# Plain 32-bit products for the first layer's queries, keys and values, in place of three products of rounded halves

## The chip, the cores and the metric

The kernel runs on one core of one Trainium2 chip. The metric is device time in microseconds of that core; the median of three runs before the change is 1491.33 us (1490.42 to 1494.95).

## The reference, cut to what matters

The reference is one inference step of a two-layer encoder for 512 prompt tokens and 64 new tokens (T = 576 rows of 1024 features). The first layer mixes tokens with eight forgetting-attention ("fox") heads and eight stick-breaking ("sb") heads of 64 features that share one input projection; the second layer uses latent attention; both are followed by a mixture of 32 experts. The change touches the input projection of the first layer alone:

```python
def ab_project(h, w_in, b_f):
    z = h @ w_in                       # (T x 1024) @ (1024 x 3080), float32
    qa, ka, va, f_logit, qb, kb, vb = jnp.split(z, cuts, axis=-1)
    logf = jax.nn.log_sigmoid(f_logit + b_f)
    ...
def sb_attend(q, k, v, pos_q, pos_k):  # 4 of 8 head pairs
    z = jnp.einsum('bqhd,bkhd->bhqk', q, k) * (HEAD_DIM ** -0.5)
    log_beta = jnp.where(before, jax.nn.log_sigmoid(z), NEG_INF)
    log_rest = jnp.where(before, jax.nn.log_sigmoid(-z), 0.0)
    later = lax.cumsum(log_rest, axis=log_rest.ndim - 1, reverse=True) - log_rest
    return jnp.einsum('bhqk,bkhd->bqhd', jnp.exp(log_beta + later), v)
```

## The kernel before

All of the work is one program of stages: the first attention (`attend` with `mla` false, from the start to about 366 us), its output product and mixture of experts, a combining stage, the latent attention, and the second mixture. Inside a stage each engine runs its own in-order list of instructions, and semaphores join them; `hold` is a wait followed by a count that every engine keeps.

`attend` takes heads two at a time: pairs 0 to 3 are stick-breaking, 4 to 7 fox. A pair is ten units (two heads by five blocks of queries, `unit_of`). For each unit TensorE computes scores, ScalarE, VectorE and GpSimd turn them into probabilities (`soften`, `softplus`, `cut`, `stick`, `exponent` for sb; `decay`, `logits`, `exponent`, `even` for fox), TensorE transposes those (`turn`), ScalarE copies the transposes out (`turn_out`), and for every two units TensorE multiplies by the values (`values`), whose result VectorE copies into `mix` (`finish`, L936). Scores run three units ahead in sb pairs and four in fox pairs.

The projections of pair p+1 are woven into pair p on TensorE (`project_ab`): `AB_AFTER` says after which unit each half of a projection stands, q0 ahead of unit 0, q1 after unit 0, k0 after 2, k1 after 3, the transposes of the keys (kt) after 4, v0 after 5, v1 after 7, the transposes of the values (vt) after 8. Each of the six product blocks is four slices of features by two halves of the 576 tokens, so 8 products of a 128x128 weight slice by 128x288 of tokens. They are made by `split_matmul`, three fp32r products: rounded weights by rounded tokens (L199), rounded weights by the low part of the tokens (L200), low part of the weights by rounded tokens (L201). The results lie in two PSUM banks, so a block of the next projection waits (`banks_free`) until ScalarE and VectorE have copied the last one out (`copy_out`: q1, k1, kt, v1, vt).

The halves come from `split`: ScalarE rounds a whole 128x1024 weight tile (`w_hi`, L189) and VectorE subtracts (`w_lo`, L193). `splits` places these after unit 1 (values of p+1), unit 4 (queries of p+2) and unit 8 (keys of p+2); so pair 6 has only the one after unit 1, and pair 7 none. The tokens are split once at the start (`split_x_hi`, `split_x_lo`). Ahead of pair 0 its own projections run with no attention beside them; the forget gates (`Gates`) use that time too.

SyncE issues the loads: `load_w(p, n)` puts a weight tile into its one buffer `wp[n]` once the tile before it has been split, and `load_past` the cached keys and values.

Of the kernel before, what the change touches and what calls it, by code (L numbers as in the profile page):

```python
# [209 lines left out]
class Gates:  # L210
# [4 lines left out]
    def __init__(self, k):  # L215
        self.k, self.nc = k, k.nc
        sem = lambda n: new_signal(k, f"g_{n}")

        flat = lambda a: a.rearrange("p j n -> p (j n)")
        room_a, room_b = flat(k.w_gu[0][0]), flat(k.w_gu[1][0])  # L220
        self.logf, self.cum, self.ones = (room_a[0:HEADS, n * KEYS:(n + 1) * KEYS] for n in range(3))
        self.low = room_a[0:HEADS, 3 * KEYS:3 * KEYS + T]
        self.t_abs, self.t_exp = (room_b[0:HEADS, n * T:(n + 1) * T] for n in range(2))
        self.t_ln = self.t_abs
        at = 2 * T
        self.tok = room_b[:, at:at + NT * HEADS].rearrange("p (t h) -> p t h", t=NT)
# [11 lines left out]
        self.out, self.tok_t, self.tok_e, self.cum_ready, self.x_hi_done, self.x_lo_done = (  # L238
            sem(n) for n in ("out", "tok_t", "tok_e", "cum_ready", "x_hi_done", "x_lo_done"))
        self.z = banks(k, 0, 2)[0:HEADS, 0:T]  # L240
        self.trans = banks(k, 2, 1)


    def load(self, sp):
        k = self.k
        sp.dma_start(self.wf, k.w_f).then_inc(self.f_in, 16)
        for b in range(2):
            sp.dma_start(k.xT[:, 4 * b:4 * b + 4, 0:T], k.x_t[:, 4 * b:4 * b + 4, :]).then_inc(self.xt_in[b], 16)
        sp.dma_start(self.bf, k.b_f).then_inc(self.f_in, 16)
# [46 lines left out]
    def products(self, pe):  # L296
        nc, k, z = self.nc, self.k, self.z
        pe.wait_ge(self.f_in, 48)
        for j in range(J):
            if j % 4 == 0:  # L300
                pe.wait_ge(self.xt_in[j // 4], 16)
            nc.tensor.matmul(z[:, 0:SEQ], self.wf[:, j, :], k.xT[:, j, 0:SEQ], start=(j == 0), stop=(j == J - 1))
            last = nc.tensor.matmul(z[:, SEQ:T], self.wf[:, j, :], k.xT[:, j, SEQ:T], start=(j == 0), stop=(j == J - 1))
        last.then_inc(self.z_ready, 1)
        pe.wait_ge(self.filled, 2)
        pe.wait_ge(self.x_lo_done, J)

# [10 lines left out]

    def split_x_hi(self, act):
        for j in range(J):  # L320
            if j % 4 == 0:
                act.wait_ge(self.xt_in[j // 4], 16)
            split_hi(self.nc, self.k.x_hi[:, j, :], self.k.xT[:, j, 0:T]).then_inc(self.x_hi_done, 1)

    def logs(self, act):
# [7 lines left out]


    def split_x_lo(self, dve):
        for j in range(J):
            dve.wait_ge(self.x_hi_done, j + 1)
            split_lo(self.nc, self.k.x_lo[:, j, :], self.k.xT[:, j, 0:T], self.k.x_hi[:, j, :]).then_inc(self.x_lo_done, 1)

# [39 lines left out]
def attend(k, mla, m, gates=None):  # L379
# [6 lines left out]
    with ExitStack() as c:  # L386
# [16 lines left out]
        else:  # L403
            wp = k.wp

            w_hi = [sb(f"w_hi{a}", [P, J, P]) for a in range(2)]
            w_lo = [sb(f"w_lo{a}", [P, J, P]) for a in range(2)]

            room = k.xT[:, :, :].rearrange("p j n -> p (j n)")
# [13 lines left out]
        else:  # L423
            names = ("zeroed hi0 hi1 hi2 lo0 lo1 lo2 kp_in0 kp_in1 vp_in0 vp_in1 cumk_in0 cumk_in1 cumq_ready projected proj_act proj_dve k_out v_out "
                     "scores_ready scored bias_ready bias_step probs_ready probsT_ready probsT_used o_ready o_done "
# [46 lines left out]
        with nc.Block() as block:  # L472
# [3 lines left out]
            def _(sp):  # L476
                row = lambda a, at: a[bass.ds(at, 1), :, :].rearrange("a p n -> p (a n)")

                def load_w(p, n):

                    if mla:
# [31 lines left out]
                def pair(p, par, kind, more):  # L513
# [23 lines left out]
                else:  # L537
                    gates.load(sp)
                    load_past(0, 0, False)
                    for n in range(3):  # L540
                        load_w(1, n)
                    store(0, 0, "sb", 0)
                    gates.store(sp)
                    store(0, 0, "sb", 1)
# [11 lines left out]
            def _(pe):  # L556
# [5 lines left out]
                def project_ab(p, par, step):  # L562
# [11 lines left out]
                    if half == 0:  # L574
                        banks_free(p, (0, 1, 3)[n], (s[f"lo{n}"], p + 1))
                    for j in range(4 * half, 4 * half + 4):
                        for b in range(2):
                            at = slice(b * HT, (b + 1) * HT)
                            last = split_matmul(nc, halves[:, b, :], (w_hi[(par + n) % 2][:, j, :], w_lo[(par + n) % 2][:, j, :]),
                                                (k.x_hi[:, j, at], k.x_lo[:, j, at]),  # L580
                                                j == 0, j == J - 1)
                    if half:
# [109 lines left out]

            def splits(split, p, par, u):

                if mla:
                    return
                last = lambda ahead: isinstance(p, int) and p + ahead >= PAIRS
                if u == 1 and not last(1):
                    split(p + 1, 1 - par, 2)
                if u == 4 and not last(2):  # L700
                    split(p + 2, par, 0)
                if u == 8 and not last(2):
                    split(p + 2, par, 1)

            def first_copies(split, copy_out, gates_part):

                if not mla:
                    split(0, 0, 0)
                    split(0, 0, 1)
                    gates_part()  # L710
                for step in copied:
                    copy_out(0, 0, step)
                    if not mla:
                        {"q1": lambda: split(0, 0, 2), "k1": lambda: split(1, 1, 0), "v1": lambda: split(1, 1, 1)}.get(step, lambda: None)()


            @block.scalar
            def _(act):
                nc.scalar.preload_act_table_set("natural_log_exp_and_others")
                if not mla:  # L720
                    gates.split_x_hi(act)
                act.wait_ge(s["zeroed"], n_zeroed)
                copy = lambda dst, src, scale=1.0: nc.scalar.activation(dst, src, ACT.Copy, scale=scale)  # L723

                def copy_out(p, par, step):
# [24 lines left out]
                    last.then_inc(s["proj_act"], 1)  # L750

                def split(p, par, n):

                    used = STEPS * (p - 1) + (2, 4)[n] if n < 2 else STEPS * p + 1
                    waits = [] if isinstance(p, int) and p == 0 and n < 2 else [(s["projected"], used)]
                    hold(act, passed, (s[f"w{n}_in"], 16 * (p + 1)), *waits)
                    split_hi(nc, w_hi[(par + n) % 2][:], wp[n][:]).then_inc(s[f"hi{n}"], 1)

# [34 lines left out]
                def pair(p, par, kind, more):  # L793
# [11 lines left out]
                    for u in range(UNITS):  # L805
# [5 lines left out]
                        copies(u)  # L811
                        splits(split, p, par, u)

                first_copies(split, copy_out, lambda: gates.logs(act))
                each_pair(act, pair)


            @block.vector
            def _(dve):
# [12 lines left out]
                dve.wait_ge(s["zeroed"], n_zeroed)  # L832
                if not mla:
                    gates.split_x_lo(dve)

# [14 lines left out]
                def copy_out(p, par, step):  # L850
# [35 lines left out]
                    if step == "q4":  # L886
                        rotate(p)

                def split(p, par, n):
                    hold(dve, passed, (s[f"hi{n}"], p + 1))  # L890
                    split_lo(nc, w_lo[(par + n) % 2][:], wp[n][:], w_hi[(par + n) % 2][:]).then_inc(s[f"lo{n}"], 1)

# [45 lines left out]
                def pair(p, par, kind, more):  # L938
# [23 lines left out]
                    for u in range(UNITS):  # L962
# [12 lines left out]
                        copies(u)  # L975
                        splits(split, p, par, u)
                    finish(p, NT - 1, kind)

                first_copies(split, copy_out, lambda: gates.sums(dve))
                if not mla:  # L980
# [1215 lines left out]
def stream_step(nc, dram):  # L2196
    with ExitStack() as ctx:
        k = Core(nc, ctx, dram)
        with ExitStack() as c:
            sb = lambda n, s, d=F32: c.enter_context(nc.sbuf_tensor(n, s, d))  # L2200
            k.wp = [sb(f"w_{n}", [P, J, P]) for n in "qkv"]
            k.wp_in = [new_signal(k, f"w_{n}_in") for n in "qkv"]
            k.x_hi, k.x_lo = sb("x_hi", [P, J, T]), sb("x_lo", [P, J, T])
            attend(k, False, None, Gates(k))
# [92 lines left out]
```

## Time and profile before

| | |
|---|---|
| median of 3 runs | 1491.33 us |
| profiled execution's own time | 1488.06 us |
| its span, first to last instruction | 1486.2 us |
| TensorE matmul busy | 1200.4 us, 81% |
| VectorE busy | 675.6 us, 45% |
| ScalarE busy | 434.9 us, 29% |
| mean granted TensorE clock | 0.92 of full speed |

The profile comes from one execution. Engines are named PE (TensorE matmul), PEld (its weight loads), DVE (VectorE), ACT (ScalarE), POOL (GpSimd) and SP (SyncE). A matmul record has a start and a modelled duration; matmuls are pipelined, so neighbouring records overlap, and the pace of a stream is read from one start to the next. A full 32-bit matmul leaves two records. "Idle before" is the time from the end of the last record on that engine to the start of this one, and what follows "<-" is what ended it; "issue" means that nothing in the profile did.

### The profile page before, as it was taken

The numbers are of one execution on the slowest core, as the hardware profiler recorded it, in microseconds if no ns is written. First come the engines' busy times: TensorE is split into PE (matmuls) and PEld (weight loads), VectorE is DVE, ScalarE is ACT, GpSimd is POOL, SyncE is SP. The second block draws the span as 40 slices with busy tenths as digits, with TensorE's granted clock in tenths as the row PEclk, the third lists the DMA queues.
The fourth block names the chain that finished last, engine by engine and source line by source line (L and its number), as shares of the span: only waits on it lengthen the run. The fifth ranks groups of instructions, "written<-read, shape, count | busy, mean of one in ns | idle before, by whom it ended". The sixth has DMA issues, their size and how long they took to land. (4 is left out here: it accounts for less than half of the span.)

```text
span 1486.2 us, 24147 instructions
## 1 busy us (share of the span) xinstructions
PE 1200.4 (81%) x8148; PEld 829.6 (56%) x8148; DVE 675.6 (45%) x1855; ACT 434.9 (29%) x985; POOL 238.0 (16%) x370
## 2 busy tenths in 40 slices
PE   6887888996994998778479699999799499777750
PEld 4766677774873554434245567676587355444420
DVE  4455664444563442222164355556656345222217
ACT  3455664335200211101022144444621021101102
POOL 1111112222012222111100000000001223112116
PEclk9999999998995999999779899999999599999985
DMA  4222123422539999999560210000033999999945
GB/s 164 75 62 72 30 95 103 160 61 77 213 142 368 376 360 380 379 373 398 189 221 1 92 70 15 29 16 15 29 133 135 366 374 355 358 378 388 394 191 189
DMA packets 61382, 290.80 MB, mean 196 GB/s; under 512 B 12689, under 2 KB 23121, under 8 KB 44257
## 3 DMA queue, kind: packets, MB, share of 16 engines
q1 hardware_dynamic: 49408, 265.90, 48.5%
q0 software_dynamic: 10560, 18.90, 4.0%
q10 hardware_dynamic: 1312, 4.72, 0.8%
q8 instruction: 56, 0.92, 0.3%
q14 instruction: 46, 0.37, 0.1%
HBM read 275.91 MB, written 29.29 MB: 205 GB/s over the span
## 5 line engine op out<-in xcount | busy, mean ns | idle before, releaser
L1745 PE MATMUL psum<-w_gu,moe_xgT 128*64 128x256 f32 x1968 | 259.8, 408 | 71.9 <-DMA w_gu<-in_w_gate_up 54.4
L1745 PEld LDWEIGHTS psum<-w_gu,moe_xgT 128*64 128x64 f32 x1968 | 153.8, 145 | 162.3 <-issue 115.2
L199 PE MATMUL psum<-x_hi,ab_w_hi 128*128 128x288 f32 x384 | 125.5, 327 | 7.4 <-ACT ab_k_tok L723 4.7
L1792 ACT ACTIVATE moe_silu<-psum 64x256 f32<-64x256 f32 x64 | 24.2, 378 | 338.8 <-PE psum L1745 294.1
L1816 DVE COPY moe_xgT<-psum 128x512 f32<-128x512 f32 x64 | 44.3, 692 | 164.1 <-PE psum L1735 163.2
L201 PE MATMUL psum<-x_hi,ab_w_lo 128*128 128x288 f32 x384 | 115.4, 301 | 0.0
L200 PE MATMUL psum<-x_lo,ab_w_hi 128*128 128x288 f32 x384 | 115.4, 300 | 0.0
L1694 POOL DMA_INDIRECT y_d<-mix,moe_slots x60 | 55.5, 925 | 363.5 <-DVE mix L1829 357.5
L1762 PE MATMUL psum<-w_dn,moe_hidT 128*64 128x512 f32 x352 | 85.1, 604 | 2.2 <-issue 2.2
L1824 DVE COPY moe_hidT<-psum 128x128 f32<-128x128 f32 x64 | 18.7, 292 | 144.3 <-PE psum L1753 142.8
L199 PEld LDWEIGHTS psum<-x_hi,ab_w_hi 128*128 128x128 f32 x384 | 74.3, 193 | 13.5 <-issue 11.8
L1797 ACT ACTIVATE mix<-psum 64x512 f32<-64x512 f32 x64 | 37.7, 589 | 134.8 <-PE psum L1762 134.8
L200 PEld LDWEIGHTS psum<-x_lo,ab_w_hi 128*128 128x128 f32 x384 | 74.1, 193 | 3.8 <-issue 2.4
L201 PEld LDWEIGHTS psum<-x_hi,ab_w_lo 128*128 128x128 f32 x384 | 73.7, 192 | 0.0
L199 PE MATMUL psum<-mix_w_hi,mix_mix_hi 128*128 128x512 f32 (+1 forms) x160 | 65.0, 406 | 9.7 <-DVE mix_w_lo L193 9.7
L1829 DVE COPY mix<-psum 64x512 f32<-64x512 f32 x64 | 44.4, 694 | 52.4 <-PE psum L1762 52.4
L632 PE MATMUL psum<-ab_kT,ab_q 128*128 128x128 f32 (+4 forms) x160 | 64.5, 510 | 4.2 <-DVE cum_tok L361 2.5
L780 ACT ACTIVATE mla_probs<-mla_score,mla_small 128x128 f32<-128x128 f32 (+4 forms) x80 | 48.3, 603 | 58.0 <-DVE mla_small L901 57.0
L201 PE MATMUL psum<-mix_w_hi,mix_mix_lo 128*128 128x512 f32 (+1 forms) x160 | 63.5, 397 | 0.0
L200 PE MATMUL psum<-mix_w_lo,mix_mix_hi 128*128 128x512 f32 (+1 forms) x160 | 63.5, 397 | 0.0
L1683 POOL DMA_INDIRECT mix<-x_d,moe_tokens x54 | 51.0, 945 | 61.0 <-issue 58.7
L632 PE MATMUL psum<-mla_kh,mla_q 96*128 96x128 f32 (+4 forms) x160 | 59.7, 479 | 0.9 <-DVE mla_q L872 0.9
(307 smaller groups left out, 2182.3 us busy)
## 6 DMA issues: line engine op xcount, KB each, us to landing
w_gu<-in_w_gate_up SPq DMA_DIRECT2D x54, 2048.0 KB, 34.9
w_dn<-in_w_down SPq DMA_DIRECT2D x44, 1024.0 KB, 36.8
xT<-in_w_down SPq DMA_DIRECT2D x20, 1024.0 KB, 40.1
w_gu<-in_w_gate_up SPq DMA_DIRECT2D x10, 1536.0 KB, 40.6
w_gu<-in_w_out SPq DMA_DIRECT2D x4, 2048.0 KB, 8.5
combine_ys<-y_d SPq DMA_DIRECT2D x16, 512.0 KB, 8.2
xT<-in_w_gate_up SPq DMA_DIRECT2D x10, 512.0 KB, 42.8
xT<-cum_d SPq DMA_DIRECT2D x8, 544.0 KB, 6.8
```

The lines of the kernel that those rows point to most:

```text
L199: nc.tensor.matmul(dst, r32(ah), r32(bh), start=first, stop=False)
L200: nc.tensor.matmul(dst, r32(ah), r32(bl), start=False, stop=False)
L201: return nc.tensor.matmul(dst, r32(al), r32(bh), start=False, stop=last)
L632: last = nc.tensor.matmul(slot(u)[0:rows, 0:min(width, BANK)], q, key[:, 0:min(width, BANK)], start=True, stop=True)
L780: nc.scalar.activation(at_unit(probs, u)[0:rows], at_unit(score, u)[0:rows], ACT.Exp, scale=-1.0, bias=small[0:rows, u % NT, 0:1], accum_o ...
L1683: pool.indirect_dma_start(out=xg[n], out_offset=None, in_=k.x_d[:, :], in_offset=bass.IndirectOffsetOnAxis(ap=idx, axis=0), bounds_check=T ...
L1694: pool.indirect_dma_start(out=k.y_d[:, :], out_offset=bass.IndirectOffsetOnAxis(ap=idx, axis=0), in_=yo[n], in_offset=None, bounds_check=2 ...
L1745: last = nc.tensor.matmul(gu(s)[h * CB:(h + 1) * CB, 0:EH], xgT[:, s, j, :], gate_up_tile(k.w_gu[n], j)[:, h * EH:(h + 1) * EH], start=(j ...
L1762: last = nc.tensor.matmul(y(s)[h * CB:(h + 1) * CB, :], hidT[:, s, j, :], w_dn[n][:, j, h * BANK:(h + 1) * BANK], start=(j == 0), stop=(j ...
L1797: nc.scalar.activation(yo[n][:, 0:BANK], y(s)[0:CB, :], ACT.Copy).then_inc(y_act, 1)
L1816: nc.vector.tensor_copy(xgT[:, s, :, :].rearrange("p j q -> p (j q)"), xtr(s)).then_inc(xgT_ready, 1)
L1829: nc.vector.tensor_copy(yo[n][:, BANK:D], y(s)[CB:P, :]).then_inc(y_dve, 1)
```

## The change

The fp32r halves of the tokens and weights go, with their buffers and semaphores. The tokens are loaded into a tile of their own, `x_in_t`, and the weights are read in `wp`, where the DMA puts them; each product is one full 32-bit matmul. A weight buffer comes free when TensorE has used it, so its reload waits for the count `projected`; the reload of the value weights moves behind the store of the keys on SyncE's queue. The gates' part on ScalarE and VectorE moves from ahead of the first copy out to behind the copy q1.

```diff
     def load(self, sp):
-            sp.dma_start(k.xT[:, 4 * b:4 * b + 4, 0:T], k.x_t[...])
+            sp.dma_start(k.x_in_t[:, 4 * b:4 * b + 4, :], k.x_t[...])
     def products(self, pe):              # the gates read k.x_in_t too
-        pe.wait_ge(self.x_lo_done, J)
-    def split_x_hi(self, act):           # both functions gone
-    def split_x_lo(self, dve):
 def attend(k, mla, m, gates=None):
-            w_hi = [sb(f"w_hi{a}", [P, J, P]) for a in range(2)]
-            w_lo = [sb(f"w_lo{a}", [P, J, P]) for a in range(2)]
                 def load_w(p, n):
-                    hold(sp, passed, (s[f"lo{n}"], p))
+                    hold(sp, passed, (s["projected"], STEPS * (p - 1) + (1, 2, 4)[n]))
                 def pair(p, par, kind, more):        # SyncE
                     load_past(p + 1, 1 - par, kind == "fox")
-                    for n in range(3):
+                    for n in range(2):
                         if not last_w:
                             load_w(p + 2, n)
                     store(p + 1, 1 - par, kind, 0)
+                    if not last_w:
+                        load_w(p + 2, 2)
                     store(p + 1, 1 - par, kind, 1)
                 def project_ab(p, par, step):        # TensorE
                     if half == 0:
-                        banks_free(p, (0, 1, 3)[n], (s[f"lo{n}"], p + 1))
+                        banks_free(p, (0, 1, 3)[n], (s[f"w{n}_in"], 16 * (p + 1)))
                     for j in range(4 * half, 4 * half + 4):
                         for b in range(2):
-                            last = split_matmul(nc, halves[:, b, :], (w_hi[...][:, j, :], w_lo[...][:, j, :]),
-                                                (k.x_hi[:, j, at], k.x_lo[:, j, at]), j == 0, j == J - 1)
+                            last = nc.tensor.matmul(halves[:, b, :], wp[n][:, j, :], k.x_in_t[:, j, at], start=(j == 0), stop=(j == J - 1))
-            def splits(split, p, par, u):            # and split() on ScalarE and VectorE
-                if u == 1 and not last(1):
-                    split(p + 1, 1 - par, 2)
-                if u == 4 and not last(2):
-                    split(p + 2, par, 0)
-                if u == 8 and not last(2):
-                    split(p + 2, par, 1)
-            def first_copies(split, copy_out, gates_part):
-                    split(0, 0, 0); split(0, 0, 1); gates_part()   # written on three lines
+            def first_copies(copy_out, gates_part):
                 for step in copied:
                     copy_out(0, 0, step)
-                        # after q1: split(0, 0, 2), after k1: split(1, 1, 0), after v1: split(1, 1, 1)
+                    if step == "q1":
+                        gates_part()
```

## Rows read from the trace of the kernel before

**Rows 1.** The page's costliest groups: line, tiles, count | busy us, mean ns | idle before

```profile
L199 PE MATMUL psum<-x_hi,ab_w_hi 128*128 128x288 f32 x384 | 125.5, 327 | 7.4 <-ACT ab_k_tok L723 4.7
...
L201 PE MATMUL psum<-x_hi,ab_w_lo 128*128 128x288 f32 x384 | 115.4, 301 | 0.0
L200 PE MATMUL psum<-x_lo,ab_w_hi 128*128 128x288 f32 x384 | 115.4, 300 | 0.0
```

**Rows 2.** TensorE's waits, pairs 0 to 3: waiting tile, releaser, total us, times, longest

```profile
PE psum L570 <- ACT ab_vT L723: 8.5, 4, 2.1
PE psum L657 <- DVE mix L936: 5.8, 4, 1.9
PE psum L644 <- ACT w_gu L777: 5.0, 4, 2.2
PE psum L199 <- ACT ab_k_tok L723: 4.7, 4, 1.2
PE psum L570 <- DVE ab_kT L877: 3.1, 4, 0.8
PE psum L644 <- ACT ab_probsT L723: 2.6, 4, 0.8
...
PE psum L632 <- DVE ab_score L920: 1.7, 4, 0.4
PE psum L644 <- issue: 1.1, 4, 0.3
```

**Rows 3.** The same view, pairs 4 to 7 (229.6 to 366.1 us)

```profile
PE psum L644 <- issue: 4.9, 8, 0.8
PE psum L657 <- DVE mix L936: 3.8, 2, 1.9
PE psum L644 <- DVE w_gu L930: 3.1, 1, 3.1
...
PE psum L570 <- DVE ab_vT L882: 0.8, 3, 0.3
```

**Rows 4.** TensorE's timeline in a product block of pair 0: start us, us

```profile
61.73 0.29 PE L200 MATMUL psum<-x_lo,ab_w_hi 128*128 128x288 f32 x1
...
64.14 0.30 PE L200 MATMUL psum<-x_lo,ab_w_hi 128*128 128x288 f32 x1
```

**Rows 5.** Timeline, full 32-bit products of the forget gates (512 and 64 columns)

```profile
16.83 1.02 PE L302 MATMUL psum<-xT,w_gu 128*8 128x512 f32 x2
17.69 0.27 PE L303 MATMUL psum<-xT,w_gu 128*8 128x64 f32 x2
```

**Rows 6.** Timeline, the latent projection: 128 columns, each with a 128x128 load

```profile
801.15 1.61 PE L2136 MATMUL psum<-mix,xT 128*128 128x128 f32 x13
```

**Rows 7.** Start of pair 0's own projections and of its scores, TensorE's timeline

```profile
38.30 0.37 PE L199 MATMUL psum<-x_hi,ab_w_hi 128*128 128x288 f32 x1 [1.63 <-DVE ab_k_tok L881]
48.91 0.35 PE L632 MATMUL psum<-ab_kT,ab_q 128*128 128x128 f32 x1 [2.54 <-DVE cum_tok L361]
```

**Rows 8.** VectorE's timeline in pair 1

```profile
108.71 1.23 DVE L193 TENSOR_TENSOR ab_w_lo<-w_v,ab_w_hi 128x1024 fp32r<-128x1024 f32 x1 [0.91 <-ACT ab_w_hi L189]
109.85 0.95 DVE L918 TENSOR_TENSOR_SCAN ab_bias<-ab_ones,ab_score 128x384 f32<-128x384 f32 x1
...
136.49 1.23 DVE L193 TENSOR_TENSOR ab_w_lo<-w_k,ab_w_hi 128x1024 fp32r<-128x1024 f32 x1 [1.37 <-ACT ab_w_hi L189]
137.63 0.28 DVE L936 COPY mix<-psum 128x128 f32 x1
```

**Rows 9.** Timeline, the last values of pair 6, which has no split after unit 8

```profile
343.93 0.80 PE L657 MATMUL psum<-ab_probsT,ab_v_all 128*64 128x64 f32 x20 [0.55 <-issue]
```

**Rows 10.** Stretches: us, busy (instructions) of PE, PEld, DVE, ACT, POOL, granted clock, DMA

```profile
94.00:98.00 4.00, 4.00 (x19) 3.82 (x19) 0.81 (x3) 2.79 (x9) 0.58 (x2) 0.57 0.72 211
...
870.00:900.00 30.00, 29.14 (x206) 20.68 (x204) 17.11 (x62) 13.79 (x40) 0.00 (x0) 1.00 0.08 20
```

More of the change, by code:

```diff
@@ L237, in __init__ @@
             sem(n) for n in ("f_in", "filled", "consts", "z_ready", "act_step", "dve_step"))
-        self.out, self.tok_t, self.tok_e, self.cum_ready, self.x_hi_done, self.x_lo_done = (
-            sem(n) for n in ("out", "tok_t", "tok_e", "cum_ready", "x_hi_done", "x_lo_done"))
+        self.out, self.tok_t, self.tok_e, self.cum_ready = (sem(n) for n in ("out", "tok_t", "tok_e", "cum_ready"))
         self.z = banks(k, 0, 2)[0:HEADS, 0:T]
@@ L301, in products @@
                 pe.wait_ge(self.xt_in[j // 4], 16)
-            nc.tensor.matmul(z[:, 0:SEQ], self.wf[:, j, :], k.xT[:, j, 0:SEQ], start=(j == 0), stop=(j == J - 1))
-            last = nc.tensor.matmul(z[:, SEQ:T], self.wf[:, j, :], k.xT[:, j, SEQ:T], start=(j == 0), stop=(j == J - 1))
+            nc.tensor.matmul(z[:, 0:SEQ], self.wf[:, j, :], k.x_in_t[:, j, 0:SEQ], start=(j == 0), stop=(j == J - 1))
+            last = nc.tensor.matmul(z[:, SEQ:T], self.wf[:, j, :], k.x_in_t[:, j, SEQ:T], start=(j == 0), stop=(j == J - 1))
         last.then_inc(self.z_ready, 1)
         pe.wait_ge(self.filled, 2)
-        pe.wait_ge(self.x_lo_done, J)
     def turn(self, pe):
@@ L316, in turn @@
         last.then_inc(self.tok_t, 1)
-    def split_x_hi(self, act):
[L320 to L323, printed above, removed]
     def logs(self, act):
@@ L539, in _ @@
                     load_past(0, 0, False)
-                    for n in range(3):
-                        load_w(1, n)
+                    load_w(1, 0)
+                    load_w(1, 1)
                     store(0, 0, "sb", 0)
+                    load_w(1, 2)
                     gates.store(sp)
@@ L691, in attend @@
             after_of = MLA_AFTER if mla else AB_AFTER
-            def splits(split, p, par, u):
-                if mla:
-                    return
-                last = lambda ahead: isinstance(p, int) and p + ahead >= PAIRS
-                if u == 1 and not last(1):
-                    split(p + 1, 1 - par, 2)
-                if u == 4 and not last(2):
-                    split(p + 2, par, 0)
-                if u == 8 and not last(2):
-                    split(p + 2, par, 1)
-            def first_copies(split, copy_out, gates_part):
[L707 to L710, printed above, removed]
+            def first_copies(copy_out, gates_part):
                 for step in copied:
                     copy_out(0, 0, step)
-                    if not mla:
-                        {"q1": lambda: split(0, 0, 2), "k1": lambda: split(1, 1, 0), "v1": lambda: split(1, 1, 1)}.get(step, lambda: None)()
+                    if step == "q1":
+                        gates_part()
             @block.scalar
@@ L719, in _ @@
                 nc.scalar.preload_act_table_set("natural_log_exp_and_others")
-                if not mla:
-                    gates.split_x_hi(act)
                 act.wait_ge(s["zeroed"], n_zeroed)
@@ L750, in copy_out @@
                     last.then_inc(s["proj_act"], 1)
[L752 to L757, printed above, removed]
                 def soften(p, u):
@@ L811, in pair @@
                         copies(u)
-                        splits(split, p, par, u)
-                first_copies(split, copy_out, lambda: gates.logs(act))
+                first_copies(copy_out, lambda: gates.logs(act))
                 each_pair(act, pair)
@@ L832, in _ @@
                 dve.wait_ge(s["zeroed"], n_zeroed)
-                if not mla:
-                    gates.split_x_lo(dve)
                 def rotate(p):
@@ L975, in pair @@
                         copies(u)
-                        splits(split, p, par, u)
                     finish(p, NT - 1, kind)
-                first_copies(split, copy_out, lambda: gates.sums(dve))
+                first_copies(copy_out, lambda: gates.sums(dve))
                 if not mla:
```

15 lines of the change are left out of this document (3 added, 12 removed).

## The prediction

> **What bounds the kernel now.** I read four views. The page's costliest groups say how much TensorE time the products take: 3 x 384 records, 356 us of modelled busy time [rows 1]; that is 8 sets of projections, each of 6 blocks of 8 products, so 24 records a block. The timeline of one block gives the real pace: 18 records from 61.73 to 64.14 us, 0.134 us each, 3.21 us a block [rows 4]. The view of who waited for whom then says who sets the end, and here the stage has two halves. In the four stick-breaking pairs (48.9 to 229.6 us, 45.2 us a pair) TensorE stands idle 32.5 us, 8.1 us a pair, and nearly every wait ends on ScalarE or VectorE [rows 2]: a chain over three engines and TensorE take turns at being last. In the fox pairs the only large waits are VectorE's copy L936 in two pairs, a latency marked "issue", and one start of pair 7 that has no projection beside it [rows 3]: TensorE is the bound, and what a product costs is paid in full. Behind 366 us nothing is touched; that part starts later or earlier as a whole.
>
> **The price of a product.** A full 32-bit product leaves two records: 512 columns take 17.69 - 16.83 = 0.86 us, 0.43 each, or 0.84 ns a column and record [rows 5]. Those weights have 8 columns. With a 128x128 load ahead of each record and only 128 columns, 13 records take 1.61 us, at most 0.124 each [rows 6], so the load is almost hidden even there. For 288 columns no row exists. By columns from [rows 5] it is 0.242 us a record; on a line between 0.124 at 128 and 0.43 at 512 it is 0.252. I take 0.244, near the first, since 512 columns leave more cover than 128 and 288 is over twice the latter. A product then takes 0.488 us against 3 x 0.134 = 0.402, a block 3.90 against 3.21: **+0.69 us a block** (0.66 to 0.82), 4.14 us a set, 33 us of TensorE over 48 blocks (32 to 39). So for TensorE alone the change is a loss; three fp32r passes were cheaper than one full product.
>
> Two rules of the Trainium skill bear on this. "TensorE: Matmul & The Clock Gate", section "Back-to-back issue gap", gives a warm single pass N/2.4 + 2.5 ns, an estimate of 122.5 ns for 288 columns; "FP8 and Floating Point Precision", section "TensorE Precision Notes", counts four passes in a true 32-bit product. By those a product goes from 368 to 490 ns, 47 us over 384 products instead of 33. The fp32r row is slower than the first rule [rows 4], so the trace disagrees with it and the sum goes by the rows.
>
> **The lead-in (pair 0's own projections, to 48.9 us).** Six blocks with nothing beside them: +4.1. Before, v0 waits 1.63 us for VectorE's key copy, which stands behind a 1.2 us split; with the split gone ScalarE's part of that copy is last, about 0.9 us after the transposes: -0.7. The first scores wait 2.54 us for the last copies of the gates [rows 7], also behind a split: -1.2 to -1.3. The gates' part now runs behind copy q1, inside the k blocks, which with 7.8 us are longer than its some 6 us (uncovered it would cost those 6). Sum **+2.1** (0 to +4.1, or -1 if the copies end earlier than I think).
>
> **Stick-breaking pairs.** ScalarE loses three roundings and VectorE three subtractions of 1.23 us in each pair. They are not idle filler: the scan of a unit starts at 109.85, right behind a subtraction that itself waited 0.91 us for its rounding, and the copy L936 at 137.63 right behind another [rows 8]. I walk once round a pair, with +0.69 at each of six blocks (+4.2 with the cold start of q0), and take off what each wait in [rows 2] gives back (it can give back 0.1 to 0.3 more than its idle time, the tail of the record before it):
> - Ahead of the first transposes (w_gu, 1.25 us a pair): its chain starts with the first scores and doesn't depend on q0; the longer q0 hides in it. -0.8.
> - kt (ab_kT, 0.78): VectorE reaches the copy some 1.2 us after k1 ends because the split after unit 1 has pushed its queue; now the copy starts at once. -0.9.
> - v0 (ab_k_tok, 1.18): the scan of unit 6 and the softening of unit 7 come after the key copies and the later scores, and so move with TensorE. -0.2.
> - Scores of unit 9 (ab_score, 0.43): behind the split after unit 4. -0.7.
> - Transposes of unit 7 (ab_probsT, 0.65): ScalarE is through with unit 7's exponent early. -0.9.
> - vt (ab_vT, 2.1): a chain of scores 9, softening, scan, cut and exponent, which has moved with TensorE by the same amount. -0.2.
> - Last values (mix, 1.45): the subtraction is gone; pair 6, which has no split after unit 8, shows what stays, 0.55 [rows 9]. -1.35, from the usual 1.9.
>
> Sum 4.2 - 5.05 = **-0.85 a pair, -3.4 for four**. Bounds: if only the first of these gives back, +3.4 a pair, +13.6; if all idle but the 0.27 "issue" and the 0.55 goes, 4.2 - 7.3 = -3.1, -12.4 for four. The walk lies between because about half of the wait time hangs on scores that TensorE now delivers later.
>
> **Fox pairs.** Pairs 4, 5 and 6 carry projections: +4.14 each. The copy L936 gives back 1.89 - 0.55 = 1.34 in pairs 4 and 5 [rows 3, 9], nothing in 6. The waits for vT (0.26) and "issue" are latencies with no block between cause and wait, and stay. Pair 7 is as before. Sum **+9.7** (9 to 12).
>
> **Queues and loads.** A weight tile is now asked for after q1, k1 or v1 instead of after its split, and is needed at the same step one pair on, most of 40 us later; the value tile is asked for behind the key store, which waits for kt and so for less than v1. I cost it at nothing; late by the whole, it would show as a wait of q0, k0 or v0 on a DMA. The start's token splits lie beside the gate products, whose end at 20.87 lets q0 go at once: nothing.
>
> **The clock.** Behind the idle time at a pair's end the granted clock falls: 94 to 98 us has 0.57, that is mostly 1.2 GHz instead of 2.4, in a q0 block; full 32-bit work with few gaps holds 1.00 in 870 to 900 us [rows 10]. So I expect no loss from the other kind of product, and perhaps one or two of these short stretches fewer. Taken as nothing.
>
> **Sum.** 2.1 - 3.4 + 9.7 = +8.4 us. The profiled execution took 1488.06 us, so 1496.5 by it; it lies 3.3 under the median shown, and against the median the forecast is 1491.3 + 8.4 = **1499.7 us**.
>
> **Rivals.**
> - *The three-engine chain was the real bound of the sb pairs and TensorE fits in entirely.* For: 8.1 us of idle time, all released by the engines relieved. Against: four of the seven waits hang on late scores. All give back: 2.1 - 12.4 + 9.7 = -0.6, 1490.7 us: no change.
> - *The same, and the clock stays up* (the one on the other side): with less idle time at the ends of pairs the cold q0 blocks go. Such a block took 4.55 us where a warm one takes 3.21, 1.3 us; four of them, and it decides once pairs 0, 1, 2 and 5 start warm: -0.6 - 5.4 = -6, 1485.3 us. Against: vt and the last values still wait.
> - *The gains are used up elsewhere*: waits only move along the units, nothing but the first gives back. 4.1 + 13.6 + 9.7 = +27 at most, 1519; typical half of the distance, 1509.
> - *The product is dearer*, 0.252 a record: TensorE +6 us more, of which the fox pairs and the lead-in show 3 and the sb pairs some: 1504. It is in the main range.
>
> **How the numbers follow.** My forecast (1494 to 1506) 0.60, TensorE fits in 0.18, that with the clock 0.10, gains used up 0.12. A measurement can tell about 0.3%, 4.5 us. Faster (under 1486.9): 0.10. Same (to 1495.8): the second case and the lower edge of the first, 0.24. Slower: 0.66. The range that leaves out two tenths: 1489 to 1511; the forecast's own is 1494 to 1506.
>
> **What would show it.** Two records of 0.24 us a product; 16 in a block of 3.9 us; fox pairs near 41.2 us where pair 4 took 38.4; no wait of the last values above 0.6; sb pairs near 44.3 us with the waits for ab_kT and ab_score gone and ab_vT near 1.7. I am wrong if a record of 288 columns takes over 0.26 or under 0.22, if sb pairs lengthen by over 1 us or shorten by over 2, if a q0 or v0 block waits for a DMA, or if the clock in the stage falls under 0.95.

## The result and the profile after

The changed kernel takes 1498.71 us (median of 10 runs, 1495.79 to 1502.80) against 1490.53 us before (10 runs, 1488.30 to 1495.21): a ratio of 1.0052, interval 1.0036 to 1.0068, or 5 to 10 us slower. The forecast was +8.4 us, and the medians differ by 8.2. The profiled executions have spans of 1486.2 and 1497.0 us. Before and after, the mean granted clock from 0 to 366 us is 0.97.

The costliest groups of the changed kernel's page that answer to [rows 1]: three weight tiles, two records a product.

```profile
L566 PE MATMUL psum<-x_in_t,w_v 128*128 128x288 f32 x256 | 65.9, 412 | 4.8 <-DVE ab_k_tok L838 3.9
L566 PE MATMUL psum<-x_in_t,w_q 128*128 128x288 f32 x256 | 67.5, 420 | 0.0
...
L566 PE MATMUL psum<-x_in_t,w_k 128*128 128x288 f32 x256 | 64.6, 406 | 1.0 <-DVE ab_q L836 1.0
```

768 records stand where 1152 stood, but the mean record lasts longer, and busy time doesn't give the pace. TensorE's timeline of the lead-in does (start us, us):

```profile
28.10 8.00 PE L566 MATMUL psum<-x_in_t,w_k 128*128 128x288 f32 x32 [1.00 <-DVE ab_q L836]
...
38.49 8.00 PE L566 MATMUL psum<-x_in_t,w_v 128*128 128x288 f32 x32 [0.89 <-ACT ab_k_tok L690]
...
49.31 0.90 PE L617 MATMUL psum<-ab_kT,ab_q 128*128 128x128 f32 x5 [1.38 <-DVE cum_tok L348]
```

32 records in 8.00 us, the last one 0.41 of it, so 31 steps in 7.59: 0.245 us a record, 0.49 a product, against 0.40 for three fp32r passes [rows 4]. The waits of 1.63 and 2.54 us of [rows 7] are now 0.89 and 1.38. TensorE's waits in pairs 0 to 3 (us in total, times, longest), to be held against [rows 2]:

```profile
PE psum L557 <- ACT ab_vT L690: 7.4, 4, 1.8
PE psum L629 <- ACT w_gu L737: 4.2, 3, 2.3
PE psum L566 <- DVE ab_k_tok L838: 3.9, 4, 1.0
PE psum L642 <- DVE mix L889: 1.4, 2, 0.7
...
PE psum L642 <- issue: 1.3, 2, 0.6
```

The waits for ab_kT, ab_probsT and ab_score are gone. The last values wait 0.6 to 0.7 us in every pair; before, they waited 1.94, 1.21, 0.78 and 1.89 us at the ends of pairs 0 to 3. The same view for pairs 4 to 7, against [rows 3]: no wait on the copy `mix` is left.

```profile
PE psum L629 <- issue: 4.9, 8, 0.8
PE psum L629 <- DVE w_gu L883: 3.5, 1, 3.5
PE psum L642 <- issue: 2.2, 4, 0.6
PE psum L557 <- DVE ab_vT L839: 0.8, 3, 0.3
```

The most telling reading is the length of each pair, from the start of one pair's first scores to the next one's, on TensorE's timeline; the lead-in is from the first product to the first scores, and pair 7 is counted to the first product of the stage behind it, where the first attention ends. All kernels of this study, in us, from one profiled execution each:

| kernel | lead-in | pairs 0 to 3 | mean | pairs 4, 5, 6 | pair 7 |
|---|---|---|---|---|---|
| before | 28.1 | 44.9 45.5 45.4 44.9 | 45.2 | 38.4 39.7 36.9 | 26.2 |
| changed | 30.2 | 45.8 44.9 45.1 45.1 | 45.2 | 43.0 40.9 40.9 | 26.6 |
| e1 all splits kept | 33.8 | 46.1 46.5 46.1 46.8 | 46.4 | 43.8 43.9 42.6 | 26.3 |
| e2 fp32r, no splits | 26.2 | 44.5 43.2 44.3 44.5 | 44.1 | 38.6 36.9 37.0 | 27.4 |
| e3 before, third split late | 29.6 | 43.6 45.9 44.7 45.4 | 44.9 | 38.3 37.4 37.3 | 26.2 |
| e4 third split kept | 31.4 | 46.3 46.4 45.9 46.5 | 46.3 | 43.5 44.2 42.6 | 26.2 |
| e5 gates first | 30.3 | 45.3 46.6 46.5 44.7 | 45.8 | 40.9 40.9 40.9 | 26.7 |
| e6 one pass | 21.8 | 42.2 42.7 42.3 41.7 | 42.2 | 26.4 26.4 26.3 | 27.8 |
| e7 products doubled | 53.5 | 64.3 64.5 64.3 64.2 | 64.3 | 64.2 64.5 64.2 | 27.4 |
| e8 before, both placed | 26.2 | 43.7 45.5 43.4 46.0 | 44.6 | 38.8 37.3 37.3 | 26.7 |
| e9 e8 and q1 early | 27.7 | 46.0 45.4 46.7 44.4 | 45.6 | 37.4 37.4 37.4 | 26.2 |
| e10 third split kept, late | 31.4 | 44.7 44.8 44.6 44.6 | 44.7 | 40.9 41.1 40.9 | 26.2 |

The changed kernel and e5 run the same work inside the pairs and still differ by 0.5 us in the mean of the first four, where their granted clocks are 0.96 and 0.93. So no smaller difference there is read from one profile.

The clock has to be read beside the lengths, because it differs between the kernels. Pairs 0 to 3 as one stretch, for the kernels before, changed, e2 and e6 (below) in this order (us, busy time of PE, PEld, DVE, ACT, POOL, granted clock, DMA share, GB/s):

```profile
48.91:229.59 180.68, 148.27 (x1073) 124.36 (x1073) 104.31 (x175) 110.46 (x240) 23.53 (x80) 0.95 0.22 68
49.31:230.18 180.87, 161.47 (x880) 116.77 (x880) 91.47 (x163) 100.53 (x228) 23.33 (x80) 0.96 0.23 69
47.02:223.53 176.51, 153.29 (x1073) 129.74 (x1073) 91.67 (x163) 101.15 (x228) 23.38 (x80) 0.90 0.24 71
42.53:211.47 168.94, 117.72 (x689) 87.83 (x689) 90.88 (x163) 99.51 (x228) 23.37 (x80) 0.79 0.24 73
```

The granted clock is either full or half, so a mean of 0.90 is a fifth of the time at the lower level (1.2 GHz in place of 2.4). What such time costs in these pairs can be estimated from e5. Its pairs 1 and 2 (46.6 and 46.5 us) had a clock of 0.90, its pairs 0 and 3 (45.3 and 44.7 us) one of 0.97, with the same work. That is 9.3 against 2.7 us at the lower level and 1.5 us of length, about a quarter of a us for each. Pairs 1 and 2 together, and pair 3:

```profile
95.33:188.36 93.03, 85.54 (x443) 62.27 (x441) 45.84 (x82) 50.59 (x114) 11.72 (x40) 0.90 0.19 58
188.36:233.01 44.65, 40.54 (x222) 29.36 (x220) 22.91 (x41) 25.14 (x57) 5.87 (x20) 0.97 0.26 85
```

### The profile page after: what moved, and what is told of

The parts are those of the page before. It is cut to its first block and busy times, and to the rows that moved or that the text cites. A ratio compares the mean times of both kernels' runs of the same rounds, so it can differ in the third digit from the quotient of the medians.

```text
span 1497.0 us, 23255 instructions
## 1 busy us (share of the span) xinstructions
PE 1227.7 (82%) x7764; PEld 816.1 (55%) x7764; DVE 643.8 (43%) x1823; ACT 408.4 (27%) x953; POOL 237.4 (16%) x370
## 5 line engine op out<-in xcount | busy, mean ns | idle before, releaser
L1768 DVE COPY moe_xgT<-psum 128x512 f32<-128x512 f32 x64 | 44.3, 692 | 163.4 <-PE psum L1687 162.2
L566 PE MATMUL psum<-x_in_t,w_v 128*128 128x288 f32 x256 | 65.9, 412 | 4.8 <-DVE ab_k_tok L838 3.9
L566 PE MATMUL psum<-x_in_t,w_q 128*128 128x288 f32 x256 | 67.5, 420 | 0.0
L1781 DVE COPY mix<-psum 64x512 f32<-64x512 f32 x64 | 44.4, 694 | 52.1 <-PE psum L1714 52.1
L566 PE MATMUL psum<-x_in_t,w_k 128*128 128x288 f32 x256 | 64.6, 406 | 1.0 <-DVE ab_q L836 1.0
L566 PEld LDWEIGHTS psum<-x_in_t,w_k 128*128 128x128 f32 x256 | 48.6, 190 | 19.1 <-issue 6.2
L566 PEld LDWEIGHTS psum<-x_in_t,w_q 128*128 128x128 f32 x256 | 50.8, 199 | 14.7
L566 PEld LDWEIGHTS psum<-x_in_t,w_v 128*128 128x128 f32 x256 | 47.4, 190 | 18.7 <-issue 6.6
## 6 DMA issues: line engine op xcount, KB each, us to landing
w_dn<-in_w_down SPq DMA_DIRECT2D x44, 1024.0 KB, 37.3
xT<-in_w_gate_up SPq DMA_DIRECT2D x10, 512.0 KB, 43.7
```

The lines of the kernel that those rows point to most:

```text
L566: last = nc.tensor.matmul(halves[:, b, :], wp[n][:, j, :], k.x_in_t[:, j, at], start=(j == 0), stop=(j == J - 1))
L1768: nc.vector.tensor_copy(xgT[:, s, :, :].rearrange("p j q -> p (j q)"), xtr(s)).then_inc(xgT_ready, 1)
L1781: nc.vector.tensor_copy(yo[n][:, BANK:D], y(s)[CB:P, :]).then_inc(y_dve, 1)
```

## The experiments

**e1: the splits kept in the changed kernel.** ScalarE and VectorE round and subtract as before, for nobody, in the lead-in too.

```diff
+                if u == 1 and not last(1):
+                    split(p + 1, 1 - par, 2)
+                if u == 4 and not last(2):
+                    split(p + 2, par, 0)
+                if u == 8 and not last(2):
+                    split(p + 2, par, 1)
```

> The changed kernel, but ScalarE and VectorE still round and subtract every weight tile at the old places (after units 1, 4 and 8), into buffers that nobody reads. This leaves only the price of the product. Theory (the extra 33 us of TensorE are half paid back by the relief of both engines): the waits of the first kernel come back on top of the longer blocks; the last values wait 1.9 us again in six pairs (+8), kt, v0 and the scores of unit 9 wait again in the four stick-breaking pairs (some +1.7 each, +7), the lead-in loses 2 us: about +17 over the changed kernel, 1515 us; stick-breaking pairs near 48 us. Rival (only the subtraction at the end of a pair ever mattered): +10, 1508 us, stick-breaking pairs near 46.5. Rival (the splits cost nothing and the product is cheap): 1499 us.

Measured: 1512.72 us, ratio to before 1.0135 (1.0117 to 1.0154), over the changed kernel by 14 us in medians and 12 by the two ratios. That lies between the theory (17) and the rival (10) and decides for neither. The price of the product alone, with no relief, is thus some 20 us. The distribution was off too: the stick-breaking pairs took 46.4 us, as the rival had it, and the fox pairs 43.8, 43.9 and 42.6, more than either.

**e2: the relief alone.** The first kernel's three passes with no split in the pairs. The two splits for pair 1 in the lead-in go too, and the weight loads wait for `projected` as in the changed kernel. One profile was taken.

```diff
             def splits(split, p, par, u):
-                if u == 1 and not last(1):
-                    ...
+                return
-                        banks_free(p, (0, 1, 3)[n], (s[f"lo{n}"], p + 1))
+                        banks_free(p, (0, 1, 3)[n], (s[f"lo{n}"], 1), (s[f"w{n}_in"], 16 * (p + 1)))
```

> The first kernel with its three fp32r passes, but without any split inside the pairs: all pairs use the halves of pair 0's weights, so queries, keys and values of the later pairs are not the right ones and only the first attention stage is read (up to the first output product at 370.9 us; behind it the routing differs). This leaves only the relief. Theory: last values wait 0.55 instead of 1.9 in six pairs (-8), the waits ab_kT, ab_score, ab_probsT of the stick-breaking pairs shrink by about 1.5 a pair (-6), lead-in -2: the stage ends near 355 us, stick-breaking pairs near 42.3, fox pairs 4 and 5 near 37.1, pair 6 as before (36.9). Rival (the chain over three engines is the bound and the splits sit in it with all of their 3.3 us a pair and more): stick-breaking pairs near 40, stage end near 347. Rival (only the last wait): stage end near 362.

Measured: the stage ends at 363.4 us, 7.5 before the first kernel's 370.9; lead-in 26.2, stick-breaking pairs 44.1, fox pairs 36.9 and 37.0 behind a 38.6. The lead-in and fox pairs 5 and 6 are as the theory said, pair 4 is not; the stick-breaking pairs gained 1.1 us each and not 2.9. The end of the stage is the one that the last rival named (362), though more than the last wait went. The waits of the stick-breaking pairs, in this kernel:

```profile
PE psum L573 <- ACT ab_vT L721: 10.6, 4, 2.8
PE psum L647 <- ACT w_gu L775: 5.0, 4, 2.2
PE psum L199 <- DVE ab_k_tok L879: 3.9, 4, 1.0
```

Waits for ab_kT, ab_score and ab_probsT are gone as in the changed kernel, and the one for ab_vT has grown from 2.1 to 2.6 us a pair: what one wait gave, the next one took in part. The clock took the rest. TensorE's idle time fell from 8.1 to 5.8 us a pair, 2.3 us, but its busy time rose from 37.1 to 38.3 us for the same work, at a granted clock of 0.90 in place of 0.95. So the relief counts for more than 1.1 us where the clock is the same: by the estimate from e5, some 2 us a pair.

**e6: the chain with little of TensorE.** One pass in place of three, on top of e2's edit.

```diff
-                            last = split_matmul(nc, halves[:, b, :], (w_hi[...], w_lo[...]), (k.x_hi[:, j, at], k.x_lo[:, j, at]), ...)
+                            last = nc.tensor.matmul(halves[:, b, :], r32(w_hi[...][:, j, :]), r32(k.x_hi[:, j, at]), start=(j == 0), stop=(j == J - 1))
```

> As the run without splits in the pairs, but one fp32r pass a product instead of three (the low parts of tokens and weights are left out, and the halves are pair 0's): a block falls from 3.21 to 1.07 us, 12.8 us a pair off TensorE. Only the first stage is read. It shows what the chain over ScalarE, VectorE and GpSimd needs by itself. Theory (about half of the wait time in the stick-breaking pairs hangs on scores that TensorE delivers late, so there are two bounds taking turns): stick-breaking pairs near 36, fox pairs near 27 as pair 7. Rival (the chain was the bound all along): stick-breaking pairs stay at 41 to 43. Stage end near 300 by the theory, near 325 by the rival.

Measured: the stick-breaking pairs 42.2 us, the fox pairs 26.4; stage end 318.3. For the first four pairs the number is the rival's: against e2, 12.8 us less of TensorE brought 1.9. In the fox pairs the same cut brought 10.5, down to the length that pair 7 has without projections. Waits in pairs 0 to 3:

```profile
PE psum L645 <- ACT ab_probsT L719: 13.8, 14, 1.7
PE psum L645 <- ACT w_gu L773: 12.7, 4, 3.5
PE psum L573 <- ACT ab_vT L719: 11.9, 4, 3.1
PE psum L573 <- DVE ab_kT L873: 8.4, 4, 2.1
```

The waits grew to 12.8 us a pair, nearly all on ScalarE's and VectorE's work. But the run doesn't show that chain alone: the granted clock in these pairs was 0.79, against 0.90 in e2, and TensorE's scores and transposes are links of the chain. By the estimate from e5, taken far beyond the clocks that it comes from, such a pair would need some 38 us at full clock, nearer to the theory than to the rival, and 12.8 us of TensorE would have brought about 4, a third. So the run decides for neither, and how long the chain is at full clock stays open.

**e7: how far that cover goes.**

```diff
-                            last = nc.tensor.matmul(halves[:, b, :], wp[n][:, j, :], k.x_in_t[:, j, at], start=(j == 0), stop=(j == J - 1))
+                            nc.tensor.matmul(halves[:, b, :], wp[n][:, j, :], k.x_in_t[:, j, at], start=(j == 0), stop=False)
+                            last = nc.tensor.matmul(halves[:, b, :], wp[n][:, j, :], nil[:], start=False, stop=(j == J - 1))
```

> The changed kernel with a second full product behind each product, of the same weights by a tile of zeros: TensorE gets 8 x 2 more records a block, +3.9 us a block, +23.4 a pair. Together with the runs of one pass, three passes and one full product it gives the price of TensorE time in a stick-breaking pair: 42.2 us with 6.4 us of product time, 44.1 with 19.2, 45.2 with 23.2. Theory (a chain over three engines bounds the pair until TensorE's own work fills it): from 23.2 to 46.6 us of product time the pair goes from 45.2 to about 65, near full price after the first 4 us. The lead-in and the fox pairs pay 23.4 each, to 53.6 and 64.3. Rival (the three-engine chain still hides a fixed share, 70%): 52 us.

Measured: 64.3 us for stick-breaking and fox pairs alike, 53.5 for the lead-in, as forecast. A fox pair grew by 64.2 - 40.9 = 23.3 us for 96 more records: 0.243 us each. With the others, product time against the length of a stick-breaking pair: 6.4 and 42.2, 19.2 and 44.1, 23.3 and 45.2, 46.6 and 64.3. One more us of TensorE costs 0.15 us in the first step, 0.27 in the second (the change), 0.82 in the third. These prices hold with the clock that came with each kernel: 0.79, 0.90, 0.96 and 1.00, higher with each step. At one clock, by the estimate from e5, they would be about 0.3, 0.6 and 0.85. Whether the longer products held the clock up or chance had a part in it was not tested.

**e3: a better place for one split in the first kernel.**

```diff
-                if u == 8 and not last(2):
+                if u == 9 and not last(2):
                     split(p + 2, par, 1)
```

> The first kernel with one line changed: the third split of a pair (keys of two pairs on) stands after unit 9 instead of after unit 8, so that VectorE's copy L936, on which the last values wait, no longer stands behind the subtraction. Theory: the wait of 1.9 us falls to 0.55 in each of pairs 0 to 5 and nothing takes its place: -1.3 each, -8 us, 1482.5 us, faster than both kernels. Rival: the rounding and subtraction now stand ahead of the next pair's first softening on ScalarE and VectorE, which starts the chain to the first transposes; in the stick-breaking pairs the wait L777 grows by 1 us and takes most of it back: -3 to -4, 1487 us.

Measured: 1485.10 us (10 runs), ratio 0.9952 (0.9932 to 0.9972), 4 to 10 us faster than before. The medians of its runs and of before's beside them (1493.6) differ by 8.5, the ratio says 7.1, so the total is the theory's 8 and not the rival's 3 to 4, though 4 lies at the edge of the interval. The profile, taken of a run 4 us above the median, shows less: pairs 4 to 6 together took 2.1 us less, where 2.7 was expected, and the first four pairs 1.1 us, where 5.3 was. In it the waits on `mix` in the fox pairs are gone (they were 3.8 us, [rows 3]) and the wait for w_gu has grown from 5.0 to 5.8 us over four pairs, a fifth of what the rival said:

```profile
PE psum L644 <- ACT w_gu L777: 5.8, 4, 2.4
...
PE psum L657 <- DVE mix L936: 1.4, 2, 0.7
```

**e4 and e10: the same work at two places in the changed kernel.** e4 keeps only the third split, after unit 8; e10 has it after unit 9. Both also keep that split's two places in the lead-in, which takes 31.4 us in place of 30.2.

```diff
 # e4
+                if u == 8 and not last(2):
+                    split(p + 2, par, 1)
 # e10
+                if u == 9 and not last(2):
+                    split(p + 2, par, 1)
```

> The changed kernel with only one of the three splits kept, the one after unit 8 (its result is read by nobody): the rounding on ScalarE and the subtraction on VectorE that stand ahead of copy L936. Theory: of the 14 us that all kept splits cost, this one is the largest part, since it puts the last values' wait from 0.6 back to 1.9 us in six pairs: +8 over the changed kernel, 1506.5 us; the waits for kt and the scores of unit 9 stay gone. Rival (in stick-breaking pairs the time at the pair's end is given back by the wait ahead of the first transposes, so only the two fox pairs pay): +3, 1501.5 us.

Measured: 1510.11 us, ratio 1.0137 (1.0115 to 1.0159): 11 us over the changed kernel in medians and 13 by the ratios, as much as the three kept splits cost in e1, and more than both theories. The last values wait 1.89 us again in fox pairs 4 and 5; behind that wait the scores that follow run at half pace. TensorE's timeline at the end of pair 4, in e4:

```profile
278.92 0.80 PE L645 MATMUL psum<-ab_probsT,ab_v_all 128*64 128x64 f32 x20 [1.89 <-DVE mix L922]
279.65 2.83 PE L620 MATMUL psum<-ab_kT,ab_q 128*128 128x128 f32 x8
```

and in the changed kernel:

```profile
272.44 0.80 PE L642 MATMUL psum<-ab_probsT,ab_v_all 128*64 128x64 f32 x20 [0.55 <-issue]
273.17 1.58 PE L617 MATMUL psum<-ab_kT,ab_q 128*128 128x128 f32 x8
```

e10 was made to tell whether that is the wait or the kept work.

> As the run that keeps the third split in the changed kernel, but after unit 9, where its subtraction no longer stands ahead of copy L936. Both engines do the same work as there. That run took 1510 us, 12 more than the changed kernel, where 1.34 us in six pairs made me expect 8; its fox pairs took 43.5, 44.2 and 42.6 us instead of 40.9, with a granted clock of 0.5 behind each pair's end. Theory (the long wait of the last values is what costs: 1.3 us itself and a slow first block of the next pair behind it): with the wait at 0.6 the clock holds at the starts of the fox pairs, they return to 40.9 us, and the time is 1500 to 1502 us. Rival (the kept work itself costs, or the slow clock there is chance): 1506 to 1510 us, with fox pairs at 42 to 44.

Measured: 1498.49 us, ratio 1.0052 (1.0036 to 1.0067): equal to the changed kernel, though both engines do the work of e4. The theory is right that the place of the split is what costs, and even its last 2 to 3 us did not come. Its timeline at the same place, and the stretches behind the ends of pairs 4 and 5, first of e4, then of e10 (us, busy time of PE, PEld, DVE, ACT, POOL, granted clock, DMA share, GB/s):

```profile
269.49 0.80 PE L645 MATMUL psum<-ab_probsT,ab_v_all 128*64 128x64 f32 x20 [0.55 <-issue]
270.23 1.58 PE L620 MATMUL psum<-ab_kT,ab_q 128*128 128x128 f32 x8
```

```profile
278.90:283.90 5.00, 4.98 (x33) 4.19 (x34) 1.52 (x11) 1.10 (x5) 2.77 (x8) 0.66 0.84 341
323.00:328.00 5.00, 4.92 (x33) 4.09 (x34) 1.49 (x10) 1.04 (x5) 2.71 (x8) 0.66 0.52 167
```

```profile
269.50:274.50 5.00, 5.00 (x40) 4.26 (x41) 2.48 (x11) 1.02 (x5) 2.54 (x7) 1.00 0.99 324
310.60:315.60 5.00, 4.98 (x40) 4.26 (x41) 2.44 (x9) 1.04 (x5) 2.54 (x7) 1.00 0.71 211
```

Fox pairs 4 to 6 take 130.3 us in e4 and 122.9 in e10, 7.4 us; the longer wait in two of them is 2.7 of it, and the remaining 4.7 is work at the lower clock level: e4's clock records have 9.5 us at half speed in these pairs, e10's none. The first four pairs differ by 6.4 us, where the two parts were not separated.

**e5: the gates' part.**

```diff
+                gates_part()
                 for step in copied:
                     copy_out(0, 0, step)
-                    if step == "q1":
-                        gates_part()
```

> The changed kernel with the gates' part of ScalarE and VectorE put back ahead of the copy q1. Both places lie beside TensorE's k blocks or q blocks, with room. Theory: no difference (1498.7 us), the lead-in stays at 30.2 us from the first product to the first scores. Rival (the part stands in the way of the copies k1 or kt in its new place): the old place is better by 1 to 2 us.

Measured: 1499.13 us, ratio to before 1.0063 (1.0046 to 1.0080), lead-in 30.3: no difference that can be told.

**e8: the first kernel's splits placed better.** The third split after unit 9, as in e3, and the lead-in's splits behind what waits for them.

```diff
-                        {"q1": lambda: split(0, 0, 2), "k1": lambda: split(1, 1, 0), "v1": lambda: split(1, 1, 1)}...
+                        {"q1": lambda: split(0, 0, 2), "kt": lambda: split(1, 1, 0)}...
                     gates.copy_turned(dve)
+                    split(1, 1, 1)
```

> The first kernel with its splits placed better: the third of a pair after unit 9 as in the earlier run, and in the lead-in the split of the next pair's queries behind the copy kt instead of ahead of it, that of its keys behind the last copies of the gates. Theory: to the 7 to 8 us of the third split's move come the 1.9 us that the lead-in gained without splits: 1481 to 1483 us, faster than both kernels. Rival: the subtraction behind the gates' copies delays the first softplus of pair 0 by what it saved; then 1483 to 1485 as the earlier run.

Measured: 1483.88 us (6 runs), ratio 0.9959 (0.9942 to 0.9975), which is the rival's number. The lead-in falls to 26.2 us as the theory had it, and pair 0 is no longer than in e3 (43.7 and 43.6), so the delay that the rival gives as its reason isn't seen. Against e3, which ran beside other runs of before, no gain can be told; e8 beats before by 4 to 9 us, e3 by 4 to 10, and both beat the changed kernel by some 14 us.

**e9: q1 ahead of unit 0, in the kernel of e8.**

```diff
-AB_AFTER = {"q0": -1, "q1": 0, ...
+AB_AFTER = {"q0": -1, "q1": -1, ...
```

> The first kernel with its splits placed better (third split after unit 9, lead-in mended), and now both halves of the next queries ahead of unit 0. With the splits placed better, TensorE waits 2.3 us a stick-breaking pair ahead of the first transposes for the chain of unit 0; q1 (3.2 us) can stand there. Theory A: it fills that wait and leaves only 1 us of delay, the chain over three engines goes on at its pace: about -1.5 us in each of four pairs, nothing in the fox pairs (no wait there): -6, 1478 us. Theory B (the stick-breaking pair is bound by the work of ScalarE and VectorE from unit 0 on, which starts later by that 1 us, as the scores of unit 3 do): no gain or 1 us lost a pair, 1484 to 1488 us.

Measured: 1485.15 us, ratio 0.9954 (0.9936 to 0.9972): no gain over e8, so theory A is out and the total is theory B's. In pairs 0 to 3 the wait for w_gu (9.1 us in e8) is gone, and in its place TensorE waits longer for ab_probsT (8.3 us, 2.6 in e8). These pairs take 45.6 us against 44.6, but at a clock of 0.93 against 0.97, and so theory B's reason is not shown apart from the clock. In e9's waits, pairs 0 to 3:

```profile
PE psum L570 <- ACT ab_vT L723: 8.5, 4, 2.1
PE psum L644 <- ACT ab_probsT L723: 8.3, 8, 1.4
```

## Why the prediction was right

**The total** came out as forecast, +8.2 of medians against +8.4, and the range held it. That it came within 0.2 us is luck: the terms of the sum, read from the two profiles, are +2.1, +0.2 and +9.7, together +12.0. One of the three was missed by 3.6 us. By its steps:

- *The product*: 0.488 us forecast, 0.486 by e7, 0.49 by the lead-in. Three fp32r passes take 0.402. In the fox pairs that are TensorE's alone the block costs (40.9 - 36.9) / 6 = 0.66 us more; 0.69 was forecast. The four passes that the Trainium skill counts ("FP8 and Floating Point Precision", "TensorE Precision Notes"), each taken at the gap that it gives for an isolated matmul ("TensorE: Matmul & The Clock Gate", "Back-to-back issue gap"), give an estimate of 0.490, and the trace agrees. The same gap makes the three fp32r passes 0.37, and there the trace, with 0.402, doesn't; so the first agreement proves little.
- *The lead-in*: +2.1 forecast, 30.2 - 28.1 = +2.1 measured; e2 splits it into +4.0 for the product and -1.9 for the relief, as the working had it (+4.1 and -2.0).
- *The fox pairs*: +9.7 forecast, and 124.8 - 115.1 = +9.7 measured. The even agreement hides a shift: pair 4 lost 4.6 and pair 5 only 1.2, because a slow stretch of the clock lies in pair 4 after and in pair 5 before. Over the three it cancels.
- *The stick-breaking pairs*: -3.4 forecast, +0.2 measured in the profile, 0.9 a pair more. This is the step that was mis-sized. Five of the seven waits moved as the walk had them (ab_kT, ab_score, ab_probsT gone, ab_k_tok 0.97 a pair, ab_vT 1.85). Two gave less. The last values gave 0.8 us a pair and not 1.35: the walk took off 1.35 "from the usual 1.9", but [rows 2] has 5.8 us over four pairs, 1.45 each, and 0.67 of it stayed. The wait ahead of the first transposes gave 0.2 and not 0.8 (5.0 to 4.2 in total). It depends on the clock of the q0 block beside it: before, it was 2.2 us in pair 3, where q0 ran at full clock, and 0.65 to 1.2 in the others; after, 1.5 in pair 3 and 0 to 2.3 in the others. The other side of the ledger moved too: TensorE's busy time rose by 3.3 us a pair and its idle time fell by 3.25. That busy time rose by less than 4.2 fits what the walk counted among the waits beyond their idle time (0.6 us) and the slightly higher clock.
- *The two halves of that step*: taken one by one they came out much smaller than in the walk, +1.1 for the product (e2 to changed) and -1.1 for the relief (before to e2), where mine were +4.2 and -5.05. The chain over the other engines is one reason: with a third of the product time a pair still takes 42.2 us (e6), though at a clock of 0.79. The other is the clock, lower in e2 than in both. At one clock they would be, by the estimate from e5, about +2.4 and -2.1. How much of each is the chain's and how much the clock's is not shown.
- *The clock*: "taken as nothing", with "perhaps one or two of these short stretches fewer". As a term it held: from the first scores to the end of pair 6, before has five stretches at the lower level, 20.5 us together, and the changed kernel three, 17.1 us; the sign of being wrong (under 0.95 in the stage) did not come. What the working left out is that the wait of 1.9 us can bring such a stretch, and that the change removes this wait. With it kept (e4) the dearer product costs 20 us, not 8. So about 12 of the us that the plain product costs are paid back by getting one split out from in front of a 0.3 us copy (e4 against e10), and e3 shows that this needs no new product.
- *Loads, gates, token splits*: nothing, as forecast; no wait on a weight DMA appears in the changed kernel's rows, and e5 shows the place of the gates' part to be free.
- *Rivals*: "TensorE fits in entirely" gave the stick-breaking pairs 42 us. They took 45.2, and only the run of one pass reached 42, so it is out. Its other form counted on four slow q0 blocks that go; two stretches fewer came, 3.4 us of slow time.

The profiles differ by 10.8 us, the medians by 8.2. The profiled execution before was 2.5 us below its median, the one after at it. The 10.8 are the +12.0 of the three terms, -1.7 because the first product starts at 19.07 us in place of 20.81, +0.4 in the last pair, whose cause stays open, and +0.1 behind it. That early start can't be put down to the change: with the changed kernel's start it stands at 20.91 us in e7, and with the first kernel's at 19.32 in e9 and 20.84 in e2. Executions of one kernel differ by several us, and the time goes with the mean clock: 1495.79 us at 0.926 and 1501.79 at 0.915 in the changed kernel's ten runs.

## What to carry to other kernels

Before trading TensorE passes for work on other engines, find out which stage each bounds: here three rounded passes were cheaper than one full product in the lead-in and in the fox pairs, which TensorE bounded, and in the stick-breaking pairs both sides of the trade counted for much less than their size. Compare kernels by busy time, idle time and clock, and not by length alone: taking work off the other engines shortened the waits in e2, and a lower clock took back half of it. Look at what a helper instruction stands in front of: moving one split behind a small copy that TensorE waits for brought 7 us, nearly what the change lost. And price a wait at the end of a burst with what the clock does behind it.

## What I had not expected of the hardware

A wait of 1.89 us instead of 0.55 ahead of the last short value products was followed by a stretch at the lower clock level in both fox pairs shown (0.66 over 5 us against 1.00). In pairs 4 to 6 the work at that level cost more than the waits themselves: 4.7 us against 2.7. e4 and e10 do the same work, and the other kernels bear it out at the ends of pairs 4 and 5. Where the wait was 1.89 us (before, e1, e4), a stretch of 3.4 us at half clock began some 1 us after it at five of six ends; the end of pair 5 in the kernel before, at 307.0 us, is the exception. Where the wait was 0.55 us (the nine other kernels), none began at any of the 18 ends. So the longer wait brings the lower clock often and not always. In the first four pairs the slow stretches also moved between kernels with the same work there (changed and e5), so there part of it is chance.
